# Feed-forward down-projection of a two-layer decoder step as seven block products for eight, on one Trainium2 core

## The chip, the core and the metric

The kernel is one program on 1 core of a Trainium2 chip. Its time is device microseconds (us) of one execution. Five engines work side by side and meet at semaphores: TensorE (PE, matrix products into PSUM), VectorE (DVE), ScalarE (ACT), GpSimd (POOL) and SyncE (SP, which issues the loads). Before the change the median of three runs is 1947.13 us (1945.86 to 1948.13).

## The reference, cut to what matters

The reference computes one inference step of two layers for 512 prompt tokens and 8 x 8 sample tokens (576 columns in all, `T`): attention in layer 0, a recurrent block in layer 1, and after each of them this feed-forward block:

```python
def conv_ffn(xn, buf, w_up, conv_w, conv_b, w_down):
    gu = xn @ w_up                                   # (T, 1024) @ (1024, 2 * 3072)
    g, u = gu[..., :D_FF], gu[..., D_FF:]
    gc, new_buf = causal_dwconv(g, buf, conv_w, conv_b)
    return (jax.nn.silu(gc) * u) @ w_down, new_buf   # (T, 3072) @ (3072, 1024)

x += conv_ffn(rmsnorm(x), ...)
```

Everything is float32. The result of the block is added to x, and x is then normalised for what follows (layer 0) or transposed and stored (layer 1).

## The kernel before

**Data.** x lies transposed in SBUF as `xT` (128 partitions x 8 chunks x 576 tokens). A product keeps float32 accuracy by splitting both factors into a high and a low part (`fp32r` tensors): `product` (L197) issues high x high, high x low and low x high into the same PSUM bank. A token row of 576 is done in two halves of 288 (`HT`), one PSUM bank each, so a weight chunk of 128 x 128 costs 6 matmuls of 288 columns.

**Weight tiles.** A weight tile is 128 x 1024 floats, that is 8 chunks of 128 x 128. SP loads tile t into ring slot t % 4 of `raw` when the tile four before is used up (`w_used`); ACT writes its high part to `whi` (`split_hi`, L167); POOL writes the low part over the raw one (`split_lo`, L191); PE takes the tile with `tile_product` (L213), 8 chunks x 6 = 48 matmuls. The accumulators are two pairs of banks, freed by DVE (`acc_free`).

**Feed-forward.** A layer's 24 chunks of the inner dimension go in three thirds of eight. In a third, PE first does 16 up tiles, a tile g and a tile u for each inner chunk (`up` in `ffn_pe`), and then 8 down tiles, one for each chunk of 128 output columns (`down`); each of these sums over the eight inner chunks of the third. For each inner chunk DVE scales g out of PSUM (`gate_out`, L1706), does the convolution (L1850 to L1855), waits for ACT's Silu (L1785), multiplies with u out of PSUM (L1861 to L1863), scales (L1867), and makes the high and the low part (L1870, L1871). In the down phase it adds each finished output chunk to `xT` (`add_x`, L301, one operation of 576 over both banks).

**What sets the order.** Every engine's list is written out by hand and is executed in that order. The first down tile of a third waits for its inner chunks one by one (`ready`), so that its first seven chunks, 42 matmuls, can run before the last inner chunk is finished. On ACT, a tile's `split_hi` stands two tiles ahead of its use (`LEAD = 2`), behind the Silu of the chunk before; POOL follows ACT.

## Time and profile before

| | us |
|---|---|
| runs, median of 3 (lowest, highest) | 1947.13 (1945.86, 1948.13) |
| profiled execution, its own time | 1946.94 |
| its span, first to last instruction | 1945.1 |
| PE busy | 1910.0 (98%) |
| DVE busy | 1071.3 (55%) |
| ACT busy | 757.0 (39%) |
| POOL busy | 701.3 (36%) |

The mean clock granted to TensorE is 0.997 of full speed. Matmuls overlap in the pipeline: one of 288 columns is recorded with about 295 ns, but the next starts some 132 ns after it, so durations of matmuls can't be added up. The busy time of an engine says nothing of what it waits for; for that one reads the timeline of the place. The idle time in square brackets behind a row of the timeline is that of its engine just before, with what ended it.

### The profile page before, as it was taken

The numbers are of one execution on the slowest core, as the hardware profiler recorded it, in microseconds if no ns is written. First come the engines' busy times: TensorE is split into PE (matmuls) and PEld (weight loads), VectorE is DVE, ScalarE is ACT, GpSimd is POOL, SyncE is SP. The second block draws the span as 40 slices with busy tenths as digits, with TensorE's granted clock in tenths as the row PEclk, the third lists the DMA queues.
The fourth block names the chain that finished last, engine by engine and source line by source line (L and its number), as shares of the span: only waits on it lengthen the run. The fifth ranks groups of instructions, "written<-read, shape, count | busy, mean of one in ns | idle before, by whom it ended". The sixth has DMA issues, their size and how long they took to land.

```text
span 1945.1 us, 36321 instructions
## 1 busy us (share of the span) xinstructions
PE 1910.0 (98%) x13285; PEld 1840.1 (95%) x13285; DVE 1071.3 (55%) x1846; ACT 757.0 (39%) x1508; POOL 701.3 (36%) x688
## 2 busy tenths in 40 slices
PE   7999999999999999999999999999989999999998
PEld 7886679999999999999999999999989999999998
DVE  3677755556555655478435325439855852542541
ACT  4555655555455554331112111247653211121121
POOL 3340013433222233443333333366544343333331
PEclk9999999999999999999999999999999999999999
DMA  5320001311111110223322223232222322322222
GB/s 149 66 56 3 25 23 44 81 35 38 44 38 37 32 46 26 71 77 86 85 78 86 82 81 86 81 104 77 66 73 77 87 80 83 86 78 84 86 76 91
DMA packets 253078, 131.47 MB, mean 68 GB/s; under 512 B 43073, under 2 KB 250754, under 8 KB 252882
## 3 DMA queue, kind: packets, MB, share of 16 engines
q1 hardware_dynamic: 252514, 128.56, 23.8%
q8 instruction: 77, 1.26, 0.3%
q10 hardware_dynamic: 444, 1.29, 0.2%
q14 instruction: 43, 0.35, 0.1%
HBM read 126.21 MB, written 3.61 MB: 67 GB/s over the span
## 4 chain that ended last, share of the span: by engine, by line
PE 86%; DVE 9%; ACT 2%; issue 2%; DMA 1%; DVEq 0%; POOL 0%; SPq 0%; ACTq 0%; POOLq 0%
PE ps L200 18%; PE ps L203 18%; PE ps L201 17%; PE ps L1225 7%; PE ps L1223 7%; PE ps L1224 7%; PE ps L1253 3%; PE ps L999 2%; PE ps L1190 2%; DVE arena L1867 1%; PE ps L232 1%; PE ps L1026 1%; PE ps L1015 1%; DVE arena L2123 1%; DVE split L1870 1%
## 5 line engine op out<-in xcount | busy, mean ns | idle before, releaser
L200 PE MATMUL ps<-split,whi 128*128 128x288 f32 x3024 | 889.4, 296 | 11.1 <-DVE split L273 4.3
L201 PE MATMUL ps<-split,whi 128*128 128x288 f32 x3024 | 885.6, 295 | 0.0
L203 PE MATMUL ps<-split,wlo 128*128 128x288 f32 x3024 | 856.2, 295 | 0.0
L194 POOL TENSOR_TENSOR wlo<-raw,whi 128x1024 fp32r<-128x1024 f32 x187 | 457.3, 2447 | 615.1 <-ACT whi L171 604.5
L200 PEld LDWEIGHTS ps<-split,whi 128*128 128x128 f32 x3024 | 568.8, 188 | 15.2 <-issue 11.9
L201 PEld LDWEIGHTS ps<-split,whi 128*128 128x128 f32 x3024 | 569.0, 188 | 0.4
L203 PEld LDWEIGHTS ps<-split,wlo 128*128 128x128 f32 x3024 | 556.2, 188 | 0.0
L171 ACT CAST whi<-raw 128x1024 fp32r<-128x1024 f32 x187 | 194.8, 1043 | 378.3 <-DMA raw<-in_ffn_w_up 225.9
L1223 PE MATMUL ps<-split,split 128*128 128x384 f32 x768 | 268.3, 349 | 0.0
L1473 DVE TENSOR_REDUCE ssq<-arena 128x16 f32<-128x1024 f32 x128 | 156.2, 1220 | 186.7 <-ACT arena L1335 186.7
L1225 PE MATMUL ps<-split,split 128*128 128x384 f32 x768 | 258.0, 336 | 0.0
L1224 PE MATMUL ps<-split,split 128*128 128x384 f32 x768 | 257.2, 335 | 0.0
L1335 ACT ACTIVATE arena<-ps 128x384 f32<-128x384 f32 (+1 forms) x384 | 174.6, 456 | 184.7 <-PE ps L1225 181.6
L1380 POOL CAST krT<-split 32x128 fp32r<-32x128 f32 x128 | 36.6, 286 | 444.1 <-DVE split L1368 295.3
L305 DVE TENSOR_TENSOR xT<-xT,ps 128x576 f32 (+1 forms) x56 | 42.3, 755 | 262.7 <-PE ps L203 262.7
L1224 PEld LDWEIGHTS ps<-split,split 128*128 128x128 f32 x768 | 144.7, 188 | 0.0
L1223 PEld LDWEIGHTS ps<-split,split 128*128 128x128 f32 x768 | 144.4, 188 | 0.1
L1225 PEld LDWEIGHTS ps<-split,split 128*128 128x128 f32 x768 | 144.2, 188 | 0.0
L1785 ACT ACTIVATE arena<-arena 128x592 f32<-128x592 f32 x48 | 33.6, 700 | 281.0 <-DVE arena L1855 281.0
L1867 DVE TENSOR_TENSOR arena<-arena,work 128x576 f32<-128x576 f32 x48 | 93.3, 1944 | 1.6
L1708 DVE TENSOR_TENSOR arena<-ps,work 128x288 f32<-128x288 f32 x56 | 25.7, 458 | 96.7 <-PE ps L203 93.8
L1861 DVE TENSOR_TENSOR arena<-arena,ps 128x288 f32<-128x288 f32 x48 | 21.8, 454 | 91.3 <-PE ps L203 78.5
(285 smaller groups left out, 2107.7 us busy)
## 6 DMA issues: line engine op xcount, KB each, us to landing
raw<-in_ffn_w_up SPq DMA_DIRECT2D x96, 512.0 KB, 3.7
raw<-in_ffn_w_down SPq DMA_DIRECT2D x48, 512.0 KB, 3.9
arena<-in_cache_ckv SPq DMA_DIRECT2D x128, 128.0 KB, 2.0
raw<-in_rec_w_in SPq DMA_DIRECT2D x16, 512.0 KB, 3.8
raw<-in_attn_w_o SPq DMA_DIRECT2D x8, 512.0 KB, 4.9
raw<-in_rec_w_out SPq DMA_DIRECT2D x8, 512.0 KB, 4.0
raw<-in_attn_w_down SPq DMA_DIRECT2D x7, 512.0 KB, 7.6
raw<-in_attn_w_uq SPq DMA_DIRECT2D x48, 64.0 KB, 2.1
```

Of the source, the lines that this page charges most:

```text
L171: act.copy(whi[:, t % RING, :], raw[:, t % RING, :]).then_inc(w_hi, 1)
L194: pool.tensor_tensor(wlo[:, t % RING, :], raw[:, t % RING, :], f32(whi[:, t % RING, :]), ALU.subtract).then_inc(w_lo, 1)
L200: pe.matmul(o, wh, a, start=first, stop=False)
L201: pe.matmul(o, wh, b, start=False, stop=False)
L203: mm = pe.matmul(o, wl, a, start=False, stop=last)
L1223: pe.matmul(ps[:, j, 0:384], ct(ct_hi, i)[:, k, :], uk[:, 0, k, col], start=(k == 0), stop=False)
L1224: pe.matmul(ps[:, j, 0:384], ct(ct_hi, i)[:, k, :], uk[:, 1, k, col], start=False, stop=False)
L1225: mm = pe.matmul(ps[:, j, 0:384], ct(ct_lo, i)[:, k, :], uk[:, 0, k, col], start=False, stop=(k == 1))
L1253: mm = pe.matmul(ps[:, 7, 0:KL + 1], s_all[par][0:n, k, :], rhs, start=(k == 0), stop=(k == SEQ_BLOCKS - 1))
L1335: act.activation(dst, src, ACT.Square).then_inc(kb_sq, 1)
L1473: dve.tensor_reduce(ssq[:, (i // 4) % 2, (i % 4) * NH:(i % 4 + 1) * NH], sqk[:, i % 2, :].rearrange("p (h e) -> p h e", e=DN), AX.X, ALU.add)\
L1867: ch(dve.tensor_tensor(hf[:, j, :], hf[:, j, :], rs[0], ALU.mult))
```

## The change

The down-projection of a third is a product of an 8 x 8 grid of weight chunks with eight inner chunks of 576 tokens. It is now done for two output chunks at a time (a **pair**, two weight tiles), as a 2 x 2 by 2 x 2 block product: output chunk 0 or 1 of the pair, inner chunks 0 to 3 or 4 to 7, and token half 0 or 1. Seven block products of 4 chunks x 3 = 12 matmuls of 288 columns take the place of eight. Here they are called M1 to M7, in the order in which PE issues them. Each needs a sum or difference of weight blocks and one of activation blocks:

- DVE forms the sums of the weight blocks of a pair (`pair_sums`), ACT their high parts (`pair_high`), POOL the low parts (`pair_low`, seven operations of 512 elements).
- For each two inner chunks (they are now k and k + 4), DVE and ACT make seven operands of 288 tokens in place of two of 576 (`first_operands`, `second_operands`).
- M1, M3, M5 and M7 go on accumulating in one bank, M2 and M4 in another. The partial sums on the way are read and added to `xT` by DVE between them (`pair_add`, seven additions of 288), and PE waits for each such reading before it goes on in that bank (`pair_pe`).

The engines' loops over thirds are written out. Semaphores of the attention part are used again: in the listings below `d_f` counts the weight sums, `d_lo` their low parts, `kr_c` the raw activation operands, `on_ps` PE's partial sums and `on_ev` the readings by DVE. Two small tensors of the recurrent block are loaded two tiles later, since their place is taken.

```diff
+        X_BANK, Y_BANK, Z_BANK = [2, 1], 0, 3
+        def pair_sums(dve, l, t0, s, p):
...
+            dve.wait_ge(w_loaded[t % RING], loaded(t) + 16 * it)
+            dve.wait_ge(w_loaded[(t + 1) % RING], loaded(t + 1) + 16 * it)
+            a11, a12 = first_half(raw, t), second_half(raw, t)
+            a21, a22 = first_half(raw, t + 1), second_half(raw, t + 1)
+            dve.tensor_tensor(s_raw[b][:, 0, :], a21, a22, ALU.add).then_inc(f_sum, 1)
+            dve.tensor_tensor(a21, a11, a21, ALU.subtract).then_inc(f_sum, 1)
+            dve.wait_ge(f_sum, SUM0 + 4 * n + 1)
+            dve.tensor_tensor(s_raw[b][:, 1, :], s_raw[b][:, 0, :], a11, ALU.subtract).then_inc(f_sum, 1)
+            dve.wait_ge(f_sum, SUM0 + 4 * n + 3)
+            dve.tensor_tensor(s_raw[b][:, 2, :], a12, s_raw[b][:, 1, :], ALU.subtract).then_inc(f_sum, 1)
+        def pair_high(act, l, t0, s, p):
...
+            split_hi(act, t, it)
+            act.wait_ge(f_sum, SUM0 + 4 * n + 3)
...
+                act.copy(s_hi0[:, 0:2, :], s_raw[b][:, 0:2, :]).then_inc(f_hi, 1)
...
+            act.wait_ge(f_sum, SUM0 + 4 * n + 4)
+            act.copy(s_hi(b, 2), s_raw[b][:, 2, :]).then_inc(f_hi, 1)
+            split_hi(act, t + 1, it)
+        def pair_low(pool, l, t0, s, p):
...
+            pool.wait_ge(f_sum, SUM0 + 4 * n + 4)
+            pool.wait_ge(w_hi, t + 1 + 4 * it)
+            half_low(first_half, t, f_lo)
+            pool.wait_ge(f_hi, HI0 + 2 * n + 1)
+            sum_low(0)
+            sum_low(1)
+            pool.wait_ge(f_hi, HI0 + 2 * n + 2)
+            sum_low(2)
+            pool.wait_ge(w_hi, t + 2 + 4 * it)
+            half_low(first_half, t + 1, f_lo)
+            half_low(second_half, t, w_lo)
+            half_low(second_half, t + 1, w_lo)
+        def pair_pe(pe, l, t0, s, p, between=None):
...
+            up_done(HK - 1, False)
+            pe.wait_ge(f_lo, LO0 + 5 * n + 1)
...
+            pair_product(pe, x, *a11, B11, every, True, True, False).then_inc(f_ps, 1)
+            pe.wait_ge(f_lo, LO0 + 5 * n + 2)
...
+            pair_product(pe, z, *s1, T1, every, True, True, False).then_inc(f_ps, 1)
+            early = range(HK - 1) if p == 0 else every
+            up_done(HK - 2, True)
+            pe.wait_ge(f_lo, LO0 + 5 * n + 3)
+            pe.wait_ge(f_ev, EV0 + 5 * n + 1)
+            mm = pair_product(pe, x, *s2, T2, early, False, True)
+            if p == 0:
+                pe.wait_ge(w_lo, t + 1 + 4 * it)
+                pe.wait_ge(acc_free[0], (t + 1 + AOFF) // 2 + 2 * it)
+                pair_product(pe, y, *a12, B21, early, True, False, False)
+                pe.wait_ge(f_lo, LO0 + 5 * n + 4)
+                pe.wait_ge(f_ev, EV0 + 5 * n + 2)
+                pair_product(pe, z, *s4, B22, early, False, False)
+                up_done(HK - 1, True)
+                mm = pair_product(pe, x, *s2, T2, range(HK - 1, HK), False, True)
+            mm.then_inc(f_ps, 1)
...
+            pair_product(pe, z, *s4, B22, range(HK - 1, HK) if p == 0 else every, False, True).then_inc(f_ps, 1)
+            pe.wait_ge(f_lo, LO0 + 5 * n + 5)
+            pe.wait_ge(f_ev, EV0 + 5 * n + 3)
+            pair_product(pe, x, *s3, T3, every, False, True).then_inc(f_ps, 1)
...
+            pair_product(pe, y, *a12, B21, range(HK - 1, HK) if p == 0 else every, p != 0, True, False).then_inc(w_used, 1)
+            pe.wait_ge(w_lo, t + 2 + 4 * it)
+            pe.wait_ge(f_ev, EV0 + 5 * n + (5 if b == 0 else 4))
+            pair_product(pe, x, *a22, T4, every, False, True).then_inc(w_used, 1)
+        def pair_add(dve, l, t0, s, p, then=None):
...
+            dve.wait_ge(f_ps, PS0 + 5 * n + 1)
+            add(0, 0, x, f_ev)
+            dve.wait_ge(f_ps, PS0 + 5 * n + 2)
+            add(1, 1, z, f_ev)
+            dve.wait_ge(f_ps, PS0 + 5 * n + 3)
+            add(0, 1, x, f_ev)
+            if then:
+                then()
+            dve.wait_ge(f_ps, PS0 + 5 * n + 4)
+            dve.wait_ge(f_ev, EV0 + 5 * n + 3)
+            add(0, 1, z, acc_free[1] if b else f_ev)
+            dve.wait_ge(f_ps, PS0 + 5 * n + 5)
+            add(1, 1, x, f_ev)
...
         def ffn_act(act, l, t0, i, nxt):
...
+                    if last and j:
+                        pair_high(act, l, t0, s, 0)
+                    act.wait_ge(f_raw, RAW0 + 6 * R + (3 if j else 1))
+                    if j == 0:
+                        act.copy(hi[:, B11, :], hf[:, 0, 0:HT]).then_inc(f_cast, 1)
+                        act.wait_ge(f_raw, RAW0 + 6 * R + 2)
+                        act.copy(hi[:, T1, :], t_raw_at(r, T1, 1)).then_inc(f_cast, 1)
+                    else:
+                        act.copy(hi[:, B21:B22 + 1, :], hf[:, 1, :].rearrange("p (a n) -> p a n", a=2)).then_inc(f_cast, 1)
+                        act.wait_ge(f_raw, RAW0 + 6 * R + 6)
+                        act.copy(hi[:, T3:T4 + 1, :], t_raw_at(r, T3, 3)).then_inc(f_cast, 1)
...
         def ffn_dve(dve, l, t0, nxt):
...
+                    if r == 3 and j:
+                        pair_sums(dve, l, t0, s, 0)
...
+            def second_operands(R, r):
...
+                dve.tensor_tensor(rw[:, T3, :], hf[:, 1, HT:T], hf[:, 0, HT:T], ALU.subtract).then_inc(f_raw, 1)
+                dve.wait_ge(f_raw, RAW0 + 6 * R + 4)
+                dve.tensor_tensor(rw[:, T2, :], rw[:, T3, :], hf[:, 0, 0:HT], ALU.add).then_inc(f_raw, 1)
+                dve.wait_ge(f_raw, RAW0 + 6 * R + 5)
+                dve.tensor_tensor(rw[:, T4, :], hf[:, 1, 0:HT], rw[:, T2, :], ALU.subtract).then_inc(f_raw, 1)
...
+                def then(p):
+                    if normed and p:
+                        norm_chunk_dve(dve, nxt, 2 * p - 2)
+                        norm_chunk_dve(dve, nxt, 2 * p - 1)
+                    if p < 3:
+                        pair_sums(dve, l, t0, s, p + 1)
```

DVE at the end of a third's up phase, before the change: from the multiplication of the last inner chunk with u to the first addition to `xT`.

```order
L1861 TENSOR_TENSOR arena<-arena,ps 128x288 [waits w_used]
L1862 TENSOR_TENSOR arena<-arena,ps 128x224
L1863 TENSOR_TENSOR arena<-arena,ps 128x64
L1866 REGISTER_ALU
L1867 TENSOR_TENSOR arena<-arena,work 128x576 [waits acc_free0]
L1870 COPY split_4608_52<-arena 128x576
L1871 REGISTER_ALU [waits f_ch]
L1871 TENSOR_TENSOR split_4608_53<-arena,split_4608_52 128x576
L305 TENSOR_TENSOR xT<-xT,ps 128x576 [waits w_used]
```

The same place now (`L1868` is the addition in `pair_add`; its first waits for M1).

```order
L2068 TENSOR_TENSOR arena<-arena,ps 128x288 [waits w_used,f_silu]
L2069 TENSOR_TENSOR arena<-arena,ps 128x224
L2070 TENSOR_TENSOR arena<-arena,ps 128x64
L2074 TENSOR_TENSOR arena<-arena,work 128x576 [waits acc_free0]
L2090 TENSOR_TENSOR arena<-arena 128x288 [waits kr_c]
L2092 TENSOR_TENSOR arena<-arena 128x288 [waits kr_c]
L2094 TENSOR_TENSOR arena<-arena 128x288 [waits kr_c]
L2096 TENSOR_TENSOR split_2016_70<-arena,split_8064_66 128x576 [waits f_cast]
L2099 TENSOR_TENSOR split_2016_70<-arena,split_8064_66 128x864 [waits f_cast]
L1868 TENSOR_TENSOR xT<-xT,ps 128x288 [waits on_ps] x3
```

Behind the scaling, one conversion and one subtraction have become three differences and two subtractions, two of which wait for ACT, and the addition that reads M1 stands behind all of them. Ahead of the last chunk's gate stand, new, the weight sums of the first pair:

```order
L2085 TENSOR_TENSOR split_2016_70<-arena,split_8064_66 128x288 [waits f_cast]
L1752 TENSOR_TENSOR arena<-raw 128x512 [waits w_loaded2,w_loaded1]
L1753 TENSOR_TENSOR raw<-raw 128x512
L1755 TENSOR_TENSOR arena<-arena,raw 128x512 [waits d_f]
L1757 TENSOR_TENSOR arena<-raw,arena 128x512 [waits d_f]
L2048 COPY arena<-fpar 128x8x2 [waits f_conv]
L1902 TENSOR_TENSOR arena<-ps,work 128x288 [waits w_used,f_ch]
```

So the gate of the last chunk (L1902) stands behind four operations that wait for the loads of two down tiles. On PE, the first pair of a third (its first matmuls of M2, M3, of the part of M6 that is drawn ahead, and of M4):

```order
L201 MATMUL ps<-split_8064_66,split_1536_73 128x288 [waits d_lo]
L202 MATMUL ps<-split_2016_67,split_1536_73 128x288
L204 MATMUL ps<-split_8064_66,split_1536_71 128x288
...
L201 MATMUL ps<-split_8064_66,split_1536_73 128x288 [waits on_ev,d_lo,f_h]
...
L201 MATMUL ps<-split_8064_66,whi 128x288 [waits acc_free0,w_lo]
...
L201 MATMUL ps<-split_8064_66,split_1536_73 128x288 [waits on_ev,d_lo]
```

The third kind of wait there, `on_ev`, is for DVE's reading of M1, and everything that was drawn ahead for the time in which the last inner chunk is not ready stands behind it.

## Rows read from the trace of the kernel before

**Rows 1.** The page's first part: busy time of each engine.

```profile
PE 1910.0 (98%) x13285; PEld 1840.1 (95%) x13285; DVE 1071.3 (55%) x1846; ACT 757.0 (39%) x1508; POOL 701.3 (36%) x688
```

**Rows 2.** Windows: a down phase of eight tiles (columns: length, then each engine's busy time).

```profile
944.30:995.00 50.70, 50.70 (x386) 50.70 (x385) 6.21 (x9) 8.40 (x8) 19.14 (x9) 1.00 0.29 83
```

**Rows 3.** Timeline of DVE (start, us, engine, line): an inner chunk, second third.

```profile
995.05 0.46 DVE L1708 TENSOR_TENSOR arena<-ps,work 128x288 f32<-128x288 f32 x1 [5.04 <-PE ps L203]
...
996.10 0.17 DVE L1847 COPY snew<-arena 128x2 f32 x1 [0.15 <-DVE arena L1711]
...
998.12 0.83 DVE L1855 SCALAR_TENSOR_TENSOR arena<-arena,fpar 128x592 f32<-128x592 f32 x1
1001.41 0.46 DVE L1861 TENSOR_TENSOR arena<-arena,ps 128x288 f32<-128x288 f32 x1 [2.46 <-PE ps L203]
...
1002.33 1.39 DVE L1867 TENSOR_TENSOR arena<-arena,work 128x576 f32<-128x576 f32 x1
```

**Rows 4.** Timeline of ACT beside it.

```profile
998.99 0.70 ACT L1785 ACTIVATE arena<-arena 128x592 f32<-128x592 f32 x1 [5.39 <-DVE arena L1855]
999.60 1.03 ACT L171 CAST whi<-raw 128x1024 fp32r<-128x1024 f32 x1
1005.29 1.05 ACT L171 CAST whi<-raw 128x1024 fp32r<-128x1024 f32 x1 [4.66 <-DMA raw<-in_ffn_w_up]
```

**Rows 5.** Timeline of DVE: first third of layer 0, its first and last chunks.

```profile
850.20 0.46 DVE L1861 TENSOR_TENSOR arena<-arena,ps 128x288 f32<-128x288 f32 x1 [0.85 <-ACT arena L1785]
...
926.05 2.98 DVE L1867 TENSOR_TENSOR arena<-arena,work 128x576 f32<-128x576 f32 x1
...
937.66 0.45 DVE L1861 TENSOR_TENSOR arena<-arena,ps 128x288 f32<-128x288 f32 x1 [0.86 <-ACT arena L1785]
...
942.32 0.76 DVE L1871 TENSOR_TENSOR split<-arena,split 128x576 f32 x1
944.35 0.76 DVE L305 TENSOR_TENSOR xT<-xT,ps 128x576 f32 x1 [1.28 <-PE ps L203]
```

**Rows 6.** Timeline of POOL beside it.

```profile
926.02 2.39 POOL L194 TENSOR_TENSOR wlo<-raw,whi 128x1024 fp32r<-128x1024 f32 x1 [6.56 <-ACT whi L171]
```

**Rows 7.** Timeline of DVE and POOL where both have work queued (recurrent block).

```profile
1355.38 1.90 DVE L2123 SCALAR_TENSOR_TENSOR arena<-arena,rpar 128x600 f32<-128x600 f32 x1
```

```profile
1354.66 1.97 POOL L2168 TENSOR_TENSOR split<-arena,split 128x576 fp32r<-128x576 f32 x1
1356.60 1.96 POOL L2168 TENSOR_TENSOR split<-arena,split 128x576 fp32r<-128x576 f32 x1
```

**Rows 8.** Single lines: duration ns minimum/median/maximum, first and last start.

```profile
L1841 DVE COPY arena<-fpar x48: 162/171/2380, 843.8 to 1873.3; 128x16 f32 x48
L1708 DVE TENSOR_TENSOR arena<-ps,work x56: 457/458/462, 845.4 to 1875.9; 128x288 f32<-128x288 f32 x56
L1451 DVE TENSOR_TENSOR arena<-arena x32: 682/702/1357, 348.9 to 780.0; 128x512 f32<-128x512 f32 x24, 128x640 f32<-128x640 f32 x8
L188 POOL TENSOR_TENSOR wlo<-raw,whi x6: 1271/1290/1356, 719.4 to 762.4; 128x512 fp32r<-128x512 f32 x6
```

**Rows 9.** Groups by line and form: busy us, mean ns of one, idle before.

```profile
L179 ACT CAST whi<-raw 128x512 fp32r<-128x512 f32 x8 | 5.1, 633 | 0.0
...
L1608 ACT CAST split<-arena 128x288 fp32r<-128x288 f32 x8 | 2.8, 430 | 11.5 <-DVE arena L1625 11.5
```

**Rows 10.** Windows at the start (length, PE busy, PEclk, DMA share, GB/s); PE's timeline.

```profile
17.00:18.00 1.00, 0.00 (x0) 1.00 1.18 299
...
19.00:20.00 1.00, 1.00 (x6) 0.50 1.21 255
...
22.00:23.00 1.00, 1.00 (x9) 0.90 0.07 1
```

```profile
18.36 0.37 PE L200 MATMUL ps<-split,whi 128*128 128x288 f32 x1 [3.87 <-DVE split L273]
```

**Rows 11.** Timeline of DVE, layer 0's last down phase: normalising.

```profile
1257.38 0.82 DVE L273 SCALAR_TENSOR_TENSOR split<-xT,rpar,split 128x576 fp32r<-128x576 f32 x1 [0.91 <-ACT split L262]
```

More of the change, by code:

```diff
@@ L1760, in ffn_pe, with fill @@
[L1760 to L1772 removed]
+            def fill(p):
+                if p < 2:
+                    tails_pe(pe, p == 1)
+                else:
+                    out_turn(pe, 2 * p)
@@ L2074, in rec_act @@
                     norm_root(act, 2)
+                    act.wait_ge(s_cst, 48)
+                    for g in range(2):
+                        act.copy(gw[:, g, 0, :, :].rearrange("p a b -> p (a b)"), gw_raw[:, g, :]).then_inc(res_h, 1)
                 if n % 2 and n >= 3:
```

308 lines of the change are left out of this document (198 added, 110 removed).

## The prediction

> **What bounds the kernel now.** I read the busy times first, then the windows of one feed-forward part, then the timelines of DVE, ACT and POOL through an inner chunk, and last the place where a third goes from up to down. PE is busy for 98% of the span [rows 1]; in the down phase it never stops: eight tiles take 50.70 us, 6.34 each, 132 ns for each of 48 matmuls [rows 2]. The other engines have room on average, DVE 55%. But the average hides a lock. A scaling (L1867) that starts at 926.05 together with a POOL operation of 2.39 us takes 2.98, ending 0.6 behind it [rows 5, 6]; a 16-element copy takes 0.16 or 2.38 us, while DVE operations that read PSUM take 457 to 462 ns always [rows 8]. So a DVE operation with SBUF operands only, and a POOL operation, run one after the other. Where both have work queued they take turns: POOL ends at 1356.63, DVE at 1357.28, 0.65 later, POOL's next at 1358.56, 1.28 later [rows 7].
>
> In the second third DVE waits 2.46 us for PE before each multiplication with u (L1861), so it has slack; in the first it starts late and waits for ACT instead [rows 3, 5]. At the end of an up phase the last chunk has little slack: L1861 at 937.66, its low part done at 943.08, and PE could do without it until 5.6 us (42 matmuls) after the last up tile, which ended at 944.3 - 6.3 = 938.0, that is 943.5 [rows 5, 2].
>
> **What is removed.** A pair had 96 matmuls and has 84. Four pairs, three thirds, two layers: 24 x 12 = 288 matmuls x 132 ns = 38.0 us. A third's down phase would be 44.4 us in place of 50.7. The row bears on matmuls with a weight load each, and those stay as they are. The Trainium skill (TensorE: Matmul & The Clock Gate, Back-to-back issue gap) gives N / 2.4 + 2.5 ns for a matmul at full clock, 122.5 ns for 288 columns, and warns that a stream with weight loads is spaced otherwise; by its formula the gain would be 35.3 us. The row says 132 ns, and I go by the row.
>
> **The up phase.** ACT used to do the next tile's split right behind the Silu [rows 4]; now the casts of the operands stand between. From the start m of the scaling, the even chunk's last cast ends at m + 1.8 (0.76, a difference of 0.45, a cast of 0.43, hand-overs of 0.1); the odd chunk's at m + 3.5 (three differences one behind the other, then a cast of 864 elements, some 0.9 between the rows of 512 and 1024) [rows 4, 8, 9]. Then come ACT's split 1.05, POOL's two low parts 2 x 2.4, during which DVE's small copies are locked out, the convolution 2.85 (996.10 to 998.95), Silu and hand-overs 0.85, multiplication 0.92 [rows 3, 4]. That is 0.92 + 1.8 + 1.0 + 4.85 + 2.85 + 0.85 = 12.3 us for an even and 13.9 for an odd chunk, against 12.7 that PE needs for two tiles. DVE falls behind by about 0.8 per two chunks, 2.75 us by the seventh chunk; the accumulators allow it about 3.7, so PE doesn't wait yet. I cost the up phase at nothing; the cover is gone beyond 3.7.
>
> **The last chunk and the first pair.** E is the end of the last up tile.
> - Before the last gate DVE now does four weight sums, 2.65 us (512 elements take 0.68 [rows 8], the next starting a little before). From m of the seventh chunk: operands to + 2.3, sums to + 5.0, a copy, gate and convolution 3.9, Silu: m + 9.9. With the lag of 2.75 the Silu ends at E + 0.85, in the first third of a layer, which starts 1 to 1.4 us late already (850.20 against 938.0 - 7 x 12.7 = 849.1 [rows 5]), at E + 2.2.
> - The split of the first down tile waited for nothing late before; now it is behind that Silu. Split 1.05, POOL's low half 1.3 (512 elements, 1.29 [rows 8]): M1 starts at E + 3.25 and M2 ends at E + 6.4.
> - M3 goes on in M1's bank, so it waits for DVE's reading of M1, and this stands behind all operands of the last chunk: six DVE operations on SBUF (scaling, three differences, two low parts), each now taking turns with one of the seven POOL operations of the pair. A POOL operation of 512 costs 1.05 when queued (1.28 for 576 [rows 7]), DVE's 0.3, 0.6 or 0.9 for 288, 576 or 864 elements. Scaling done at E + 3.8, differences at 5.15, 6.5 and 7.85, low parts at 9.5 and 11.5, the reading at 12.0. PE idles from 6.4 to 12.0. What was drawn ahead for this time stands behind the same wait and fills nothing.
> - From M3 on PE needs 4.6 us to the end of M5 and M6's rest at E + 18.6, but M7 waits for the reading of M5, and this for the weight sums of the next pair, that DVE begins at 16.5: M7 starts at 20.0 and ends at E + 21.6, where 11.1 was due. That is 10.5 us lost.
> - Without the lock the same chain ends with the reading of M1 at E + 6.0 (below); that POOL does all seven first would put it at about 14.5. These are the bounds; rows 7 speak for turns.
>
> **The other pairs.** In pair 1 and 2 sums, readings and low parts fit: M3 ends 4.8 us after the start, the sums (POOL's last operation first, up to 1.3) end at 9.0, two readings at 9.7, M7 is due at 9.5: 0.1 to 0.2 each. The low half for the next M1 is ready 1.3 after the sums, before 11.1. So a third costs 50.7 - 6.3 + 10.5 + 0.3 = 55.2 us, 4.5 more than before. Six thirds: + 27; two first thirds x 1.35 us: + 3.
>
> **The clock.** At the start PE idles for 3.87 us before 18.36, and from 19 to 22 the granted clock is 0.50 of full, 1.2 GHz in place of 2.4; at 22 to 23 it is back [rows 10]. It cost some 3.2 us at half speed, 1.6 us. The gap of 5.6 us in each third is longer than that one, so I take 6 x 1.6 = + 10; 0 if it doesn't fall, 19 if the gap before M1 counts too.
>
> **Normalising in layer 0.** In the last third two operations of 0.82 us [rows 11] stand ahead of the sums of pair 1 and 2, each taking turns with POOL, so that M7 waits 2 to 3 us more in both: + 5 (bounds 1.4 and 8). The moved loads of the recurrent block (two casts of 1.05 and two POOL operations of 2.4, which had been done ahead of it and now lie in its first 20 us of PE work) I cost at 0; some 2 us if not covered. At the end of the kernel one reading of 0.46 stands in place of 0.76: -0.3.
>
> **Sum.** 27 + 3 + 10 + 5 = + 45 us. The profiled execution took 1946.94 us (span 1945.1), 0.2 from the median of 1947.13, so the forecast is **1992 us**, 2.3% slower. Bounds of its terms: reading of M1 2.5 us later (+ 15), clock 0 to 19 (-10 to + 9), lag 0 in place of 0.85 to 2.2 (-9), normalising -4 to + 3: 1965 to 2018.
>
> **Rivals.**
> - *The lock does not bite at the first pair* (other end). The place is the six DVE operations behind E, the price 6 us a third, and it decides from the point where the reading of M1 comes by E + 7.5. Then there is no lag, the Silu ends ahead of E, M1 starts at E + 0.4, multiplication 0.92, operands to 5.6, reading at 6.0: M7 ends at 15.7, a third takes 15.7 + 33.4 = 49.1, 1.6 less than before; x 6 and 1.5 back for normalising: 1939. The gap would be 2.5 us, so the clock holds. Rows 5 to 8 speak against it; for it speaks only that durations on POOL are rough.
> - *The stall is absorbed altogether*, since operands come early enough or PE gets past: all of the 38 us but short waits, 1909 to 1925. The order of DVE and PE speaks against it: before, 5.4 us passed from L1861 to the low part, and M1 and M2 are only 3.2.
> - *The up phase falls behind too.* If one more POOL operation of 2.4 us is waited for in every two chunks, DVE loses 9.6 us in a third, of which 3.7 less the 2.75 already used are free: some 6 us x 6 more, 2028. For it: the odd chunk's copy and POOL's start are 0.1 us apart. Against: the chain above already holds both POOL operations.
> - *The products are no faster for being fewer*, if groups of 12 with a new bank each cost something at their seams: 1.0 us per pair would be + 24. In the down phase before, PE changes banks every 24 matmuls within the 132 ns of rows 2, so I give it little.
>
> **Chances.** Forecast with its range 0.62; up phase behind 0.13; seams 0.04; lock harmless 0.11; absorbed 0.07; the rest between, about 1947, 0.03. A measurement of this kernel can tell a difference of 0.2%, 4 us, from none. Faster by more 0.18, within it 0.04, slower 0.78. For 8 in 10 I leave out what is absorbed and the worst of the up phase: 1937 to 2024.
>
> **What would show it.** PE should show two gaps at the start of each third's down phase, of about 3 and 5 us, the first ended by POOL's low half, the second by DVE's addition to `xT`, then a short one before M7; six thirds alike. DVE's last operands should alternate with POOL's 512-element operations, each difference taking 1.2 to 1.4 us in place of 0.45. The granted clock should dip in six places. DVE's wait for PE before L2068 (the old L1861) should be gone by the middle of each up phase. Matmul spacing stays 132 ns. I am wrong if the second gap is under 2 us or the up phases themselves get longer than 101 us.

## The result, and the profile after

The changed kernel takes 1991.52 us (median of 4 runs, 1990.49 to 1992.30), the kernel of before 1947.60 us (4 runs, 1945.86 to 1948.13): a ratio of 1.0227, 95% interval [1.0209, 1.0245]. The forecast was 1992. The total fits to half a microsecond, but its terms do not fit that well: some of them were off by 2 to 5 us, and the misses cancelled. The profiled execution took 1991.96 us (span 1989.9), against 1946.94 (span 1945.1) before, so 44.8 us of span are to be explained.

The busy times of the changed kernel, to be held against [rows 1]:

```profile
PE 1893.2 (95%) x12997; PEld 1816.0 (91%) x12997; DVE 1242.3 (62%) x2158; ACT 849.5 (43%) x1652; POOL 803.3 (40%) x808
```

PE has 288 matmuls fewer, as counted. Its busy time fell by 16.8 us only, where 288 matmuls at 132 ns are 38.0, in part because many of those left ran at the lower clock. PE now stands still for 96.7 us in place of 35.1. What it waited for, by the view of its waits (total us, times, longest):

```profile
PE ps L201 <- DVE xT L1868: 53.5, 19, 7.0
```

L1868 is DVE's addition of a bank to `xT`, the reading. There was no such wait before. PE's timeline in the second third of layer 0 (start, us, engine, line; in brackets the idle time ahead of the instruction and what ended it) shows the four places, the starts of M1, M3, M5 and M7 of pair 0:

```profile
1095.63 0.37 PE L201 MATMUL ps<-split,whi 128*128 128x288 f32 x1 [0.88 <-issue]
...
1106.04 0.58 PE L201 MATMUL ps<-split,split 128*128 128x288 f32 x1 [6.98 <-DVE xT L1868]
...
1113.59 0.37 PE L201 MATMUL ps<-split,whi 128*128 128x288 f32 x1 [0.25 <-DVE xT L1868]
...
1116.86 0.38 PE L201 MATMUL ps<-split,whi 128*128 128x288 f32 x1 [1.04 <-DVE xT L1868]
```

The wait before M3 is 6.97 to 6.99 us in all six thirds. That is a chain that always has the same length, not a chance meeting. DVE and POOL in the same place:

```profile
1094.86 0.45 DVE L2068 TENSOR_TENSOR arena<-arena,ps 128x288 f32<-128x288 f32 x1 [2.41 <-PE ps L204]
...
1095.77 1.62 DVE L2074 TENSOR_TENSOR arena<-arena,work 128x576 f32<-128x576 f32 x1
1097.42 1.44 DVE L2090 TENSOR_TENSOR arena<-arena 128x288 f32<-128x288 f32 x1
1098.90 1.41 DVE L2092 TENSOR_TENSOR arena<-arena 128x288 f32<-128x288 f32 x1
1100.34 1.40 DVE L2094 TENSOR_TENSOR arena<-arena 128x288 f32<-128x288 f32 x1
1101.66 1.82 DVE L2096 TENSOR_TENSOR split<-arena,split 128x576 fp32r<-128x576 f32 x1
1103.41 2.12 DVE L2099 TENSOR_TENSOR split<-arena,split 128x864 fp32r<-128x864 f32 x1
1105.45 0.81 DVE L1868 TENSOR_TENSOR xT<-xT,ps 128x288 f32<-128x288 f32 x2
```

```profile
1094.26 1.27 POOL L1782 TENSOR_TENSOR wlo<-raw,whi 128x512 fp32r<-128x512 f32 x1 [14.93 <-ACT whi L172]
1095.48 4.51 POOL L1779 TENSOR_TENSOR split<-arena,split 128x512 fp32r<-128x512 f32 x3
1099.95 4.66 POOL L1782 TENSOR_TENSOR wlo<-raw,whi 128x512 fp32r<-128x512 f32 x3
```

The six DVE operations between L2068's group and the reading last 1.62, 1.44, 1.41, 1.40, 1.82 and 2.12 us, where their sizes alone would give about 0.76, 0.46, 0.46, 0.46, 0.75 and 1.06. Each waits for one of POOL's seven operations and then goes: a POOL operation ends at 1096.77, DVE's scaling at 1097.39, POOL's next at 1098.55, DVE's first difference at 1098.86, and so on. POOL's seven end at 1104.6, DVE's six at 1105.5. The readings themselves have one operand in PSUM and stay at 0.45 us: rows of that kind do not take part. The Trainium skill (SBUF — State Buffer, Who interferes with whom) says that a DVE instruction with two SBUF inputs contends with a GpSimd instruction that reads SBUF, that one with at most one SBUF input, outside its faster modes, does not, and that the port pair they share is an exclusive lock. The trace agrees, 1.40 to 1.44 us against 0.45; what it adds is that these two queues, both with work pending, take turns one for one.

The clock, by windows of PE over the same stretch (length, PE busy, granted clock, DMA share, GB/s):

```profile
1098.00:1101.00 3.00, 1.05 (x8) 1.00 0.05 16
1101.00:1104.00 3.00, 0.00 (x0) 0.63 0.00 0
1104.00:1107.00 3.00, 0.96 (x4) 0.50 0.00 0
1107.00:1110.00 3.00, 3.00 (x14) 0.50 0.00 0
1110.00:1113.00 3.00, 3.00 (x17) 0.66 0.00 0
1113.00:1116.00 3.00, 2.57 (x18) 1.00 0.00 0
```

PE stops at about 1098.9. The granted clock is at 0.50 (1.2 GHz) when M3 starts, and back at full only after 1112. The 33 matmuls from M3 to M5 take 7.55 us, less 0.25 of waiting, where 4.36 were due at 132 ns: 2.9 us lost. Over five thirds the stretch takes 6.40 to 7.55 us, so the loss is 1.8 to 2.9 us.

The other pairs are as cheap as forecast. A pair takes 11.35 us (DVE's readings of M1 at 1118.73, 1130.08 and 1141.43), that is 84 matmuls of 132 ns and 0.25 us before M7.

Where the 44.8 us arise, by the same events in both traces:

| stretch | longer by, us |
|---|---|
| up to layer 0's feed-forward part (L1742, now L1936) | -1.5 |
| its first third, up to the first gate (L1708, now L1902) of the second | +5.9 |
| its second third | +6.95 |
| its last third, with normalising | +13.2 |
| recurrent block | +4.0 |
| layer 1: first, second, last third | +5.8, +6.97, +3.5 |

In layer 0's last third the clock fell once more, which the second third has not: M7 of pair 1 starts at 1289.22 behind a wait of 2.58 us, and from 1289.5 to 1293 the granted clock is 0.50.

### The profile page after: what moved, and what is told of

It is laid out like the page before. It is cut to its first block, busy times and chain, and to the rows that moved or that the text cites. A ratio compares the mean times of both kernels' runs of the same rounds, so it can differ in the third digit from the quotient of the medians.

```text
span 1989.9 us, 35277 instructions
## 1 busy us (share of the span) xinstructions
PE 1893.2 (95%) x12997; PEld 1816.0 (91%) x12997; DVE 1242.3 (62%) x2158; ACT 849.5 (43%) x1652; POOL 803.3 (40%) x808
## 4 chain that ended last, share of the span: by engine, by line
PE 85%; DVE 10%; ACT 2%; issue 1%; POOL 1%; DMA 1%; SPq 0%; DVEq 0%; ACTq 0%; POOLq 0%
PE ps L201 18%; PE ps L204 17%; PE ps L202 17%; PE ps L1225 7%; PE ps L1223 7%; PE ps L1224 7%; PE ps L1253 3%; PE ps L999 2%; PE ps L1190 1%; PE ps L233 1%; DVE arena L2354 1%; PE ps L1026 1%; PE ps L1015 1%; DVE split L2099 1%; DVE split L2096 1%
## 5 line engine op out<-in xcount | busy, mean ns | idle before, releaser
L201 PE MATMUL ps<-split,whi 128*128 128x288 f32 x2640 | 784.3, 298 | 29.8 <-DVE xT L1868 11.6
L202 PE MATMUL ps<-split,whi 128*128 128x288 f32 x2640 | 778.3, 296 | 0.0
L204 PE MATMUL ps<-split,wlo 128*128 128x288 f32 x2640 | 760.9, 296 | 0.0
L201 PEld LDWEIGHTS ps<-split,whi 128*128 128x128 f32 x2640 | 499.9, 189 | 39.1 <-issue 34.5
L202 PEld LDWEIGHTS ps<-split,whi 128*128 128x128 f32 x2640 | 500.0, 189 | 0.4
L195 POOL TENSOR_TENSOR wlo<-raw,whi 128x1024 fp32r<-128x1024 f32 x139 | 338.6, 2451 | 396.9 <-ACT whi L172 386.2
L204 PEld LDWEIGHTS ps<-split,wlo 128*128 128x128 f32 x2640 | 492.2, 189 | 0.0
L1782 POOL TENSOR_TENSOR wlo<-raw,whi 128x512 fp32r<-128x512 f32 x96 | 127.3, 1351 | 186.7 <-DVE arena L1757 97.1
L1868 DVE TENSOR_TENSOR xT<-xT,ps 128x288 f32<-128x288 f32 x168 | 73.5, 452 | 157.0 <-PE ps L204 156.7
L1224 PEld LDWEIGHTS ps<-split,split 128*128 128x128 f32 x768 | 144.7, 188 | 0.0
L1223 PEld LDWEIGHTS ps<-split,split 128*128 128x128 f32 x768 | 144.3, 188 | 0.1
L1225 PEld LDWEIGHTS ps<-split,split 128*128 128x128 f32 x768 | 144.1, 188 | 0.0
L201 PE MATMUL ps<-split,split 128*128 128x288 f32 x304 | 94.3, 313 | 46.0 <-DVE xT L1868 41.9
L201 PEld LDWEIGHTS ps<-split,split 128*128 128x128 f32 x304 | 60.2, 198 | 48.8 <-DVE split L2099 43.1
```

What stands on the lines that cost most here:

```text
L195: pool.tensor_tensor(wlo[:, t % RING, :], raw[:, t % RING, :], f32(whi[:, t % RING, :]), ALU.subtract).then_inc(w_lo, 1)
L201: pe.matmul(o, wh, a, start=first, stop=False, skip_group_check=resumed)
L202: pe.matmul(o, wh, b, start=False, stop=False, skip_group_check=resumed)
L204: mm = pe.matmul(o, wl, a, start=False, stop=last, skip_group_check=resumed)
L1223: pe.matmul(ps[:, j, 0:384], ct(ct_hi, i)[:, k, :], uk[:, 0, k, col], start=(k == 0), stop=False)
L1224: pe.matmul(ps[:, j, 0:384], ct(ct_hi, i)[:, k, :], uk[:, 1, k, col], start=False, stop=False)
```

## Experiments

Ratios are to the kernel of before, which ran on the same chip between the others; "gain" is the difference from the changed kernel's 1991.5 us. The experiments were measured in three groups; the kernel of before took 1947.2, 1947.8 and 1947.5 us in them, so gains of different groups compare to about half a microsecond.

### Is it the alternation of DVE and POOL?

```diff
-pool.tensor_tensor(s_lo_op[b][:, i, :], s_raw[b][:, i, :], f32(s_hi(b, i)), ALU.subtract)
+w = slice(0, 16 if p == 0 else 512)
+pool.tensor_tensor(s_lo_op[b][:, i, w], s_raw[b][:, i, w], f32(s_hi(b, i))[:, w], ALU.subtract)
...
+            if p == 0:
+                a11, a12, s3, a22, s1, s2, s4 = [(v[0], v[0]) for v in (a11, a12, s3, a22, s1, s2, s4)]
```

> For the first pair of each third POOL makes only 16 of 512 columns of each low part, and TensorE takes the high parts in place of the low ones as weights, with as many matmuls: what is left out is the low part of these weights. All else of the change stays. Theory A (DVE and POOL taking turns makes up more than half of the wait before M3): DVE's six operations of 9.8 us shrink to the 4.5 to 5.5 us that the same shapes take elsewhere, the wait of 6.98 us becomes 2.5 us, the clock holds, and the 0.9 us before M1 goes: 6 x (4.4 + 2.4 + 0.9) = 46 us less, about 1946 us, the kernel of before or just under it. Theory B (the chain of dependences between DVE and ACT is the wait, and the turns only stretch what would wait anyway): the wait stays over 5.5 us and the time over 1975 us.

Measured: 1955.97 us, ratio 1.0048 [1.0030, 1.0066], gain 35.5; the kernel leaves out the low parts of these weights, so it is for measuring only. The same DVE operations as above, in this kernel:

```profile
1091.20 0.76 DVE L2079 TENSOR_TENSOR arena<-arena,work 128x576 f32<-128x576 f32 x1
1091.99 0.46 DVE L2095 TENSOR_TENSOR arena<-arena 128x288 f32<-128x288 f32 x1
1092.49 0.46 DVE L2097 TENSOR_TENSOR arena<-arena 128x288 f32<-128x288 f32 x1
1092.98 0.46 DVE L2099 TENSOR_TENSOR arena<-arena 128x288 f32<-128x288 f32 x1
1093.35 0.77 DVE L2101 TENSOR_TENSOR split<-arena,split 128x576 fp32r<-128x576 f32 x1
1094.41 1.06 DVE L2104 TENSOR_TENSOR split<-arena,split 128x864 fp32r<-128x864 f32 x1 [0.29 <-ACT split L1988]
```

and PE behind them, at M3 and M5:

```profile
1095.98 0.38 PE L201 MATMUL ps<-split,split 128*128 128x288 f32 x1 [2.56 <-DVE xT L1873]
...
1102.37 0.37 PE L201 MATMUL ps<-split,whi 128*128 128x288 f32 x1 [0.24 <-DVE xT L1873]
```

From L2079 to the reading the chain takes 4.2 us in place of 9.7, the wait before M3 is 2.56 in place of 6.98, and the one before M1 is gone. So the alternation makes 4.4 of the 7.0 us. The rest is the plain chain of operands behind which the reading stands. The gain fell 10 us short of what I expected. One reason is in the two rows: from M3 to M5 6.39 us pass, 1.8 more than 33 matmuls at 132 ns and 0.24 of waiting, so the clock still falls behind a wait of 2.56 us here. It falls in four of the six thirds, and the length of the wait does not say in which: in the last third of layer 0, behind 2.40 us, M3 to M5 take 4.84 us, and in the second third of layer 1, behind a shorter wait, they take 6.39:

```profile
1745.08 0.38 PE L201 MATMUL ps<-split,split 128*128 128x288 f32 x1 [2.24 <-DVE xT L1873]
...
1751.47 0.37 PE L201 MATMUL ps<-split,whi 128*128 128x288 f32 x1 [0.24 <-DVE xT L1873]
```

### Is the clock a cost of its own?

```diff
+            if p == 0:
+                for i in range(40):
+                    pe.matmul(ps[:, 5, 0:HT], s1[0][:, 0:P], t_hi_op[:, 0, T1, :], start=i == 0, stop=i == 39)
```

> 40 further matmuls of 288 columns on a bank that nobody reads stand between M2 and M3 of each pair 0: 5.3 us of work at 132 ns, in a wait of 6.98 us. Nothing else differs. Theory A (the granted clock falls because TensorE stands still there, and costs 1.8 to 2.95 us a third behind the wait): the clock stays at 1.00, the 33 matmuls from M3 to M5 take 4.4 us again in place of 6.4 to 7.6, and the kernel gains 6 x 2.4 = 14 us: 1977 us. Theory B (the low clock there is nothing that the wait made, or the matmuls hold up something): 1991 us or more.

Measured: 1980.29 us, ratio 1.0175 [1.0157, 1.0193], gain 11.2, with 240 matmuls more than the changed kernel. PE, the filling first, then M3 and M5:

```profile
1097.81 5.49 PE L1832 MATMUL ps<-split,split 128*128 128x288 f32 x40
...
1105.07 0.37 PE L201 MATMUL ps<-split,split 128*128 128x288 f32 x1 [1.77 <-DVE xT L1871]
...
1109.92 0.37 PE L201 MATMUL ps<-split,whi 128*128 128x288 f32 x1 [0.24 <-DVE xT L1871]
```

From M3 to M5 4.85 us pass in place of 7.55, and the granted clock is 1.00 in each window of 3 us from 1094 to 1109. M3 starts as late as ever, 11.07 us behind the start of the last multiplication against 11.18; only its speed differs. So theory A holds, at 11 us where 14 were expected. The filling does not keep the clock up everywhere: in the first and the last third of layer 1 it falls to 0.50 all the same, behind the same wait of 1.77 us:

```profile
1608.30 0.37 PE L201 MATMUL ps<-split,split 128*128 128x288 f32 x1 [1.77 <-DVE xT L1871]
...
1614.69 0.37 PE L201 MATMUL ps<-split,whi 128*128 128x288 f32 x1 [0.24 <-DVE xT L1871]
```

And in two other thirds DVE gets its scaling done ahead of POOL's second operation, so that M3 starts 0.8 to 1.0 us earlier behind the multiplication than in the changed kernel, which is no matter of the clock. So 11.2 us is not the exact price. By the spacing of M3 to M5 in the changed kernel it is 1.6 to 2.9 us a third (the sixth against the same place in the kernel of the experiment before), 13.4 in all: between a quarter and a third of the excess.

### Where the reading stands

```diff
                 dve.tensor_tensor(rw[:, T3, :], hf[:, 1, HT:T], hf[:, 0, HT:T], ALU.subtract).then_inc(f_raw, 1)
+                read(0)          # xT += bank of M1, in the last chunk of a third only (comments added here)
                 dve.tensor_tensor(rw[:, T2, :], rw[:, T3, :], hf[:, 0, 0:HT], ALU.add).then_inc(f_raw, 1)
+                read(1)          # xT += bank of M2
                 dve.tensor_tensor(rw[:, T4, :], hf[:, 1, 0:HT], rw[:, T2, :], ALU.subtract).then_inc(f_raw, 1)
```

> DVE reads M1 and M2 of pair 0 into xT between its sums of the last chunk (after T3's difference and after T2's sum), not behind all of its operands, so that TensorE may begin M3's first three steps, and those of M7's bank and of M4, some 6 us earlier. Theory A (the reading stands in the wrong place): the 27 matmuls of these three products, 3.6 us at full clock, move into the wait of 6.98 us before M3, DVE's chain gets no shorter, two readings of 0.8 to 1.5 us are only moved: about 3 us a third at the old clock and up to 1.5 us more where the clock falls less, so 1964 to 1974 us, with two shorter waits in place of the one. Theory B (the operands' chain alone sets the end of pair 0, and the readings, now under the lock, lengthen it): within 3 us of 1991.5 us or above.

Measured: 1964.01 us, ratio 1.0091 [1.0073, 1.0109], gain 27.5. PE in the second third: M3's first steps, then M6's, then M7:

```profile
1096.23 0.37 PE L201 MATMUL ps<-split,split 128*128 128x288 f32 x1 [0.33 <-DVE xT L1866]
...
1099.81 0.40 PE L201 MATMUL ps<-split,whi 128*128 128x288 f32 x1 [2.14 <-POOL wlo L1782]
...
1108.29 0.37 PE L201 MATMUL ps<-split,whi 128*128 128x288 f32 x1 [1.04 <-DVE xT L1876]
```

Theory A. Moving two readings of 0.45 us costs nothing, and 27 matmuls that had been drawn ahead for this wait can now really be in it. From M1 to M7 15.8 us pass in place of 21.2. A new wait appears, 2.14 us for POOL's low part of a12, because POOL's seven operations are what takes longest once DVE is out of the way. This is the cheapest repair: no work was removed. The clock still falls in all six thirds, behind the two waits of 0.33 and 2.14 us with 9 matmuls between them; in the second third it is at 0.50 from 1100.2 to 1103.7.

### Starting POOL earlier

```diff
+                    if last and j:
+                        pair_high(act, l, t0, s, 0)
                     act.wait_ge(S["conv"], l * FC + s * TF + r * 2 + j + 3)
                     act.activation(cb[:, j, 0:CBN], cb[:, j, 0:CBN], ACT.Silu).then_inc(S["silu"], 1)
-                    if last and j:
-                        pair_high(act, l, t0, s, 0)
```

> ACT makes the high parts of pair 0's weights and sums ahead of the last chunk's Silu, so that POOL can begin its seven operations (10.4 us from 1094.26 to 1104.6 us in the second third) some 2 to 3 us earlier. Theory A (the lock is a fixed amount of POOL time, and each microsecond of it moved ahead of the last chunk's multiplication, where DVE waits for TensorE anyhow for 2.4 us, is saved): the wait before M3 shrinks by 1 to 2 us and the 0.9 us before M1 goes: 6 x 2 to 3 us less, 1974 to 1981 us. Theory B: Silu comes 3.5 us later, TensorE's last up tile is done by then, and DVE multiplies later: no gain or up to 6 x 1 us more, 1991 to 1998 us.

Measured: 1978.34 us, ratio 1.0162 [1.0143, 1.0180], gain 13.2: theory A. POOL begins its seven at 1086.84 and ends them at 1097.4. DVE's timeline shows what pays for it:

```profile
1088.16 1.57 DVE L2057 TENSOR_SCALAR arena<-arena,fpar 128x592 f32<-128x592 f32 x1
1089.77 1.74 DVE L2059 SCALAR_TENSOR_TENSOR arena<-arena,fpar 128x592 f32<-128x592 f32 x1
1091.54 1.74 DVE L2062 SCALAR_TENSOR_TENSOR arena<-arena,fpar 128x592 f32<-128x592 f32 x1
1094.05 0.46 DVE L2068 TENSOR_TENSOR arena<-arena,ps 128x288 f32<-128x288 f32 x1 [0.77 <-ACT arena L1974]
```

The convolution's three operations now alternate with POOL and take 5.1 us in place of 2.3. DVE had 2.4 us to spare there, waiting for PE, so much of this is free. The multiplication then waits for the Silu, and starts 1.65 us after M1 (M1 started at 1101.28 - 5.71 - 3.17 = 1092.40) in place of 0.77 before it; but from there to the reading of M1 it is 6.6 us in place of 10.6. The lock costs what the locked-out engine did not have to wait for anyway.

### Two smaller terms: normalising, and the recurrent block

```diff
                 for p in range(4):
-                    pair_add(dve, l, t0, s, p, lambda: then(p))
+                    pair_add(dve, l, t0, s, p, lambda: then(p), lambda: mid(p))   # mid: chunk 2p - 2, behind the reading of M2
+                    if normed and p in (1, 2):
+                        norm_chunk_dve(dve, nxt, 2 * p - 1)
```

> The changed kernel with one edit: in the last third of layer 0 the two normalising operations of DVE do not stand between the reading of M3 and the sums of the next pair; one stands behind the reading of M2, the other behind the last reading of the pair. Theory A (they made M7 wait 2.58 and 2.39 us in pair 1 and 2): both waits go to 0.3 or less, 4.5 us less, 1987 us. Theory B (the wait only moves to M1 or M3 of the next pair): 1991 us, with a new wait there.

Measured: 1990.67 us, ratio 1.0235 [1.0217, 1.0252], a gain of 0.8, within what can be measured. In the changed kernel M7 waits in pair 1 and 2 of that third:

```profile
1289.22 0.37 PE L201 MATMUL ps<-split,whi 128*128 128x288 f32 x1 [2.58 <-DVE xT L1868]
...
1304.52 0.37 PE L201 MATMUL ps<-split,whi 128*128 128x288 f32 x1 [2.39 <-DVE xT L1868]
```

and with the edit they are 1.74 us (M7 at 1288.00) and 3.19 (at 1302.55): 4.93 us in sum in place of 4.97. The waits have the size of the forecast term (5), the place was not the cause: neither theory names it rightly. The clock falls once in this stretch in either kernel, behind the longer of the two waits. Before, the sums (L1752 to L1757) ran at 0.68 us each, but late; now they start early, while POOL still has its own operations, and alternate with them. The overlap stays, and the edit only decides in which pair it is paid.

```diff
-                if t == REC0 + 1:
+                if t == REC0 + 3:
...
-            act.wait_ge(s_gw, 32)
-            for g in range(2):
-                act.copy(gw[:, g, 0, :, :].rearrange("p a b -> p (a b)"), gw_raw[:, g, :]).then_inc(res_h, 1)
...
                     norm_root(act, 2)
+                    act.wait_ge(s_gw, 32)
+                    for g in range(2):
+                        act.copy(gw[:, g, 0, :, :].rearrange("p a b -> p (a b)"), gw_raw[:, g, :]).then_inc(res_h, 1)
```

> The kernel of before with one part of the change alone: the gate weights of the recurrent block are loaded two tiles later, and their two casts on ACT and two low parts of 2.4 us on POOL are done inside the recurrent block, not ahead of it. Theory A (this is why the stretch from the recurrent block's first gate to the second feed-forward part is 4.0 us longer in the changed kernel): 1951 us, with waits of PE for POOL's low parts in the first 40 us of that stretch, as in the changed kernel at 1318.72 (0.98 us). Theory B (what I took in the forecast: covered): 1947 us, and the 4 us come from elsewhere.

Measured: 1949.44 us (11 runs), ratio 1.0011 [1.0002, 1.0020]: 1.7 to 2.1 us, between the two theories. Its trace has three short waits early in the recurrent block that the kernel of before has not: 0.45 us at 1314.84, 0.48 at 1317.19 and 0.62 at 1324.44, each for a low part of POOL. The changed kernel has the same three (0.46, 0.48 and 0.63 us, at 1339.50, 1341.85 and 1349.11), and one more ahead of them that this part alone does not make:

```profile
1318.72 0.40 PE L201 MATMUL ps<-split,whi 128*128 128x288 f32 x1 [0.98 <-POOL wlo L195]
```

It follows POOL's last low parts and additions of layer 0, which pile up at the end of the down phase. In the table this wait belongs to layer 0's last third, since the recurrent block is counted there from its first gate, at 1329.33. From that gate to layer 1's feed-forward part the kernel of before takes 174.78 us, this one 178.35 and the changed kernel 178.80, so by the traces the moved loads make 3.6 of the 4.0 us. By the times of 11 runs they make about 2. The two measures differ by 1.5 us, and that stays open.

### Together

> Both edits of order together: DVE reads M1 and M2 among its sums of the last chunk, and ACT makes the high parts of pair 0 ahead of the last Silu. Alone they gave 27.5 and 13.2 us. Theory A (they take away different things): with the first alone a third still waits 0.9 us before M1 and 2.1 us for POOL's low part of a12, both because POOL ends its seven operations late; with the second, POOL ends 4 us earlier and both waits go. Left are 0.3, 0.24 and 1.04 us a third, and the clock holds: 6 x (9.15 + 2.4 - 1.6) = 60 us less than the changed kernel, 1932 us, up to 1940 if the Silu, now behind four casts, costs a microsecond a third; faster than the kernel of before. Theory B (the gains only add, or overlap, since both shorten the same wait): 1951 us or more.

The edits are those of "Where the reading stands" and "Starting POOL earlier". Measured: 1954.68 us, ratio 1.0047 [1.0032, 1.0063], gain 36.8. That is theory B, and my 1932 was wrong by 23. PE at M3 and M5:

```profile
1096.28 0.37 PE L201 MATMUL ps<-split,split 128*128 128x288 f32 x1 [2.55 <-DVE xT L1866]
...
1102.67 0.37 PE L201 MATMUL ps<-split,whi 128*128 128x288 f32 x1 [0.24 <-DVE xT L1876]
```

I had counted the reading as early, as in the kernel with the first edit, without following it. It stands behind DVE's multiplication, scaling and first difference, and these now come 1.5 us after M1 has started, since the Silu is late, where M1 had followed the multiplication before. So M1 and M2 are done ahead of the reading again. The clock also falls again (0.77 and 0.66 in the windows from 1096 to 1102).

```diff
                 pe.wait_ge(f_ev, EV0 + 5 * n + 2)
                 pair_product(pe, z, *s4, B22, early, False, False)
+                pe.wait_ge(w_lo, t + 1 + 4 * it)
+                pe.wait_ge(acc_free[0], (t + 1 + AOFF) // 2 + 2 * it)
+                pair_product(pe, y, *a12, B21, range(1), True, False, False)
...
-            pair_product(pe, y, *a12, B21, range(HK - 1, HK) if p == 0 else every, p != 0, True, False).then_inc(w_used, 1)
+            pair_product(pe, y, *a12, B21, range(1, HK) if p == 0 else every, p != 0, True, False).then_inc(w_used, 1)
```

> Three edits of order: the two of the kernel with both, the normalising operations of layer 0 (L273/L274 of DVE) moved out of the place ahead of the next pair's sums, and in pair 0 nine of M6's twelve matmuls kept back until after M5, in place of three, so that they cover the 1.04 us that M7 waits for the reading of M5. Theory A: 6 x 0.8 us and 4.5 us less than with the first two edits alone, 1922 to 1930 us. Theory B (what M6 no longer fills ahead of the last operands is waited for there): only the 4.5 us of the normalising.

Measured: 1947.96 us (10 runs), ratio 1.0006 [0.9997, 1.0015], 6.7 us better than with two edits. The wait before M7 went from 1.03 to 0.24 us in each third; the normalising waits are 1.75 and 3.19 us, as with that edit alone. The 6 x 0.8 us came, the 4.5 us for the normalising did not; the other 1.9 us of the gain I did not trace. From M3 to M5 it is 5.60 us behind a wait of 2.83 in the first third of layer 0, and 4.36 behind one of 2.72 in the second third of layer 1: the clock falls in three of the six thirds.

```diff
                     dve.wait_ge(acc_free[q], (t + 7) // 2 + 1 + 2 * it)
+                    if r == 3 and j:
+                        pair_read(dve, l, t0, s, 0, 0)
                     dve.tensor_tensor(hf[:, j, :], hf[:, j, :], rs[0], ALU.mult).then_inc(f_raw, 1)
...
+                for i in range(16):          # in the first of the two kernels only (comment added here)
+                    pe.matmul(ps[:, 5, 0:HT], s1[0][:, 0:P], t_hi_op[:, 0, T1, :], start=i == 0, stop=i == 15)
                 up_done(HK - 1, True)
```

> The kernel with the three edits of order (1948 us), carried on: DVE reads M1 ahead of the last chunk's scaling, so that M3 can follow M2 at once, in place of 2.4 to 2.8 us later; of DVE's normalising operations the first stands behind the reading of M5; and 16 matmuls of 288 columns on a bank that nobody reads stand ahead of the last chunk's steps, where PE would wait for DVE's last operand some 2.8 us. Theory A: DVE's chain of operands, whose end the reading does not move, now alone sets M5, some 6.7 us behind the end of M2; that is what the second third has already, but four of the six thirds took 8.2 to 8.5 us, by the clock: 4 x 1.7 = 7 us less, and 2 to 3 us less for the normalising: 1936 to 1943 us, faster than the kernel of before by a quarter of a per cent or more. Theory B (the wait moves and the clock falls as before, whatever stands in it): 1945 to 1950 us.

> The same kernel without the 16 matmuls. Theory A (the wait costs nothing by itself, since DVE's last operand sets M3's last step either way, but the clock falls in it): PE waits 2.5 to 3 us before M3's last step, and the 39 matmuls behind it take up to 2 us more in some thirds: 3 to 10 us over the kernel with them. Theory B (the clock doesn't matter at a wait of this length): the same time within 2 us.

Measured: with the filling 1949.01 us, ratio 1.0012 [1.0003, 1.0021]; without it **1943.70 us, ratio 0.9979 [0.9970, 0.9988]** (11 runs), the only kernel here that beats the one of before, by 0.2%. Both expectations missed, and for one reason. (1949 lies in the range of theory B, but the clock does not fall in any of the six thirds, as that theory has it.) With the reading of M1 early, PE's standing still is cut in two by itself: it waits for the reading of M2 and then for DVE's last operand. The starts of M4, M3's last step, M5 and M7 without the filling:

```profile
1097.15 0.37 PE L201 MATMUL ps<-split,split 128*128 128x288 f32 x1 [1.20 <-DVE xT L1866]
...
1099.96 0.40 PE L201 MATMUL ps<-split,split 128*128 128x288 f32 x1 [0.98 <-DVE split L2112]
1101.26 0.37 PE L201 MATMUL ps<-split,whi 128*128 128x288 f32 x1 [0.24 <-DVE xT L1876]
...
1104.52 0.37 PE L201 MATMUL ps<-split,whi 128*128 128x288 f32 x1 [0.24 <-DVE xT L1876]
```

The granted clock stays at 1.00 in all windows of 3 us from 1090 to 1105, and in the other five thirds too. There was nothing for the filling to save, and it takes 2.29 us where the wait is 0.98, so it was on the path: from M4 to M5 4.98 us pass with it and 4.11 without, 0.87 us a third and 5.3 us more in all. I had sized it for one wait of 2.8 us. Most of what this kernel has over the one with three edits is the clock: from the start of DVE's last multiplication to M5 it takes 8.33 us, where the other takes 8.55 in the thirds that keep the clock and 9.8 in those that lose it.

## Why the prediction was right

The mechanism was right: a reading in the middle of an accumulation, queued behind all operands of the last chunk, each of them alternating with POOL, in all six thirds. The rivals fell: a harmless lock (the six stretched operations; that a gap of 2.5 us would leave the clock up, as that rival has it, is not borne out either, since it fell behind waits of 2.24 to 2.56 us in four thirds of the kernel without POOL's low parts, and in the kernel of before behind one of 2.37 at 163.71), absorption (waits of 7 us), seams between groups (12 matmuls take 1.585 us, 132 ns each), and an up phase that falls behind. Two of its sums do not come out as written: its terms give 1969 as the lower bound, not 1965, and in the rival of the up phase 9.6 us less the 0.95 still free are 8.65 a third, not 6. Neither changes the account. By its steps, for the second third:

- *288 matmuls x 132 ns.* Counted and spaced as forecast.
- *The up phase lags by 0.8 us in two chunks, 2.75 by the seventh.* Wrong: there is no lag that PE or DVE shows. DVE still waits for PE before its multiplications, 1.95 us at 1069.42 and 2.41 at 1094.86, where I had named the end of that wait as a sign. From one multiplication to the next, behind an odd chunk, 12.74 us pass (1069.42 to 1082.16), where I had worked out 13.9, and 1.08 of them are DVE's wait for PE at the gate. DVE's copies were not both shut out by both of POOL's operations, and hand-overs took 0.03, not 0.1:

```profile
1076.70 0.29 DVE L2054 COPY snew<-arena 128x2 f32<-128x2 f32 x1
1076.91 0.17 DVE L2055 COPY snew<-arena 128x16 f32<-128x16 f32 x1
1076.99 2.66 DVE L2057 TENSOR_SCALAR arena<-arena,fpar 128x592 f32<-128x592 f32 x1
```

  POOL's two ran from 1074.55 to 1079.33. Had I kept to alternation here too, the copies would have had their turn between them. Both copies ran there, and it was the convolution's first operation that waited for POOL's second.
- *M1 at E + 3.25.* Measured E + 0.9, with E, the end of the last up tile, at 1094.75, since without the lag the Silu is early. The size was off by 2.35 us.
- *Reading of M1 at E + 12.0.* Measured E + 11.1 to 11.3. From the end of the scaling to that of the last low part I had worked out 7.7 us of turns, and 8.1 were measured. This sets the path, so that the error in M1 made no difference but in the wait: 7.0 where I had 5.6.
- *M7 at E + 20.0, and 1.6 us of clock.* Measured E + 22.1, of which 21.6 was forecast. The clock was under-sized: 2.9 us in this third, 13.4 in all by the spacing, and 11.2 by the kernel that keeps it up in four thirds, where I had 10. Without it M7 would be at E + 19.2, a little ahead of the forecast. The wait before M7, 1.04, was forecast at 1.4.
- *Pairs 1 and 2, 0.1 to 0.2 each.* Measured 0.25.
- *First thirds 1.35 dearer.* Wrong, with the lag: they are a microsecond cheaper than the second, +5.9 and +5.8 against +6.95 and +6.97. Some 0.7 of this is the clock: M3 to M5 take 6.82 and 6.66 us there, against 7.55 and 7.35. The rest, which lies before the down phase, I did not trace.
- *Normalising + 5.* Measured 4.97 us of waits, some 1.6 us of clock behind the first of them, and 1.0 at 1318.72 for POOL; with M3 to M5 1.15 us shorter than in the second third, these add up to 13.4, where +13.2 was measured. *Moved loads 0*, with some 2 if not covered: measured 2 by the times, 3.6 by the trace. The recurrent block in all + 4.0.
- *The last third.* Layer 1's costs 3.5, not 6.1: the transposes and output work between M3 and M4 cover M7's wait, which is missing there.

Second thirds came to 6.95 where 4.5 + 1.6 = 6.1 stood in the sum, first thirds to 5.8 where 7.5 stood. The half microsecond of agreement is luck. What was not luck is which chain was followed.

## What to carry to other kernels

Before a product may go on in a bank that another engine must first read, ask what stands ahead of that reading in the reader's queue. 27 matmuls had been drawn ahead to fill this place and stood behind the same wait; moving two readings of 0.45 us forward gave 27.5 us, the most of any single edit that leaves the result whole (35.5 came from leaving out POOL's low parts, which does not). Where two engines alternate on SBUF operands, count the other's queue into each operation, and place the other's work where the first one waits anyway. And a saving of 38 us in matmuls was worth 4 us when all was done, mostly because each third has one place where DVE's last operand, not PE, sets the time: the second third, first gate to first gate, took 152.6 us before, 6.3 us of matmuls went, and the best kernel takes 150.4.

## What the runs showed of the hardware

- With DVE operations on two SBUF operands in one queue and POOL's in the other, the two take turns one for one, down to 288 elements: 0.46 us become 1.40 to 1.44, and a POOL operation of 512 elements stretches from 1.28 us to 1.5. Operations that read PSUM keep their 0.45 us in between. Short copies do not keep to it: two of them ran back to back between two POOL operations (1076.70 and 1076.91).
- The granted clock fell in all six thirds behind the wait of 6.98 us. Behind shorter single waits their length did not decide: it fell behind 1.77 (with the filling ahead of it), 2.05, 2.24 and 2.56 us, and stayed up behind 1.77 (the same), 2.40, 2.72 and 2.80, in the same place of other thirds or of other kernels. The 2.05 is from the first third of layer 1 and the 2.80 from its last, both in the kernel with two edits. What decides it no run here shows. The loss came after the wait: 1.6 to 2.9 us behind 6.98, 1.2 to 1.8 behind the short ones.
- With two waits of 1.2 and 1.0 us and 12 matmuls between them the clock stayed up in all six thirds, in the one trace of that kernel. Nobody ran the filling against an uncut short wait, so what cutting and filling are worth beside each other is open.
- Going on in a bank whose partial sum had just been read costs PE nothing beyond the wait for the reading: 132 ns a matmul there as elsewhere.
